# Weighted one-hot factors of the first prompt tile on GpSimd between its gathers, those of the second tile on VectorE

## The reference

```python
s1 = jnp.einsum('nhd,kd->nhk', q[..., :half], c1)
s2 = jnp.einsum('nhd,kd->nhk', q[..., half:], c2)
...
e = jnp.take_along_axis(cidx, si, axis=-1)
g = jax.nn.softmax(sv, axis=-1)
ue = u[e]
ve = v[e]
a = jax.nn.gelu(jnp.einsum('nhkd,nd->nhk', ue, hx), approximate=False)
return jnp.einsum('nhk,nhkd->nd', (g * a), ve)
```

## Time and the profile before

| | |
|---|---|
| median of 3 runs | 1579.57 us (1575.74 to 1583.34) |
| the profiled execution | 1577.69 us, its span 1575.9 us |
| PE busy | 1167.5 us (74%) |
| DVE busy | 1035.7 us (66%) |
| POOL busy | 646.8 us (41%) |
| ACT busy | 291.7 us (19%) |
| moved by DMA | 434.92 MB, mean 276 GB/s |

### The profile page before, as it was taken

One profiled execution on the slowest core, in us unless ns is written; L12 is line 12 of the kernel. 1 busy time (PEld: TensorE's weight loads), 2 busy tenths in 40 slices (PEclk: granted clock), 3 DMA queues, 4 the chain that ended last, 5 costly groups with the idle time before them and its releaser, 6 DMA issues.

```text
span 1575.9 us, 12501 instructions
## 1 busy us (share of the span) xinstructions
PE 1167.5 (74%) x4129; PEld 695.2 (44%) x4129; DVE 1035.7 (66%) x2220; ACT 291.7 (19%) x701; POOL 646.8 (41%) x565
## 2 busy tenths in 40 slices
PE   7999998975420683674586584027799999999998
PEld 3444444852110673673244374026544444444443
DVE  2436313579999878777447569999856566666664
ACT  2024501210000011111046441149600000000000
POOL 1110000333333757767324453445544454444451
PEclk9999999997755555555698777556799999999999
DMA  7654231684643988998987765656699999999996
GB/s 265 219 187 164 81 143 44 250 293 161 250 140 97 358 275 325 364 339 282 389 296 250 253 228 202 228 175 208 233 409 410 409 410 409 409 409 410 409 401 252
DMA packets 155361, 434.92 MB, mean 276 GB/s; under 512 B 14592, under 2 KB 36496, under 8 KB 155040
## 3 DMA queue, kind: packets, MB, share of 16 engines
q0 software_dynamic: 74688, 271.66, 46.8%
q1 hardware_dynamic: 80608, 162.45, 28.3%
HBM read 427.72 MB, written 6.34 MB: 275 GB/s over the span
## 4 chain that ended last, share of the span: by engine, by line
PE 56%; DVE 21%; DMA 9%; ACT 8%; issue 3%; POOL 3%; SPq 1%; DVEq 0%; ACTq 0%
PE wide L1189 28%; DVE rows_ring L1505 6%; PE accumB L873 5%; PE accumA L873 4%; DMA ring<-in_w_in 3%; DMA rows_ring<-in_peer_u,expert 3%; ACT hot L805 3%; POOL rows_ring L576 2%; PE wide L1079 2%; PE accumB L1101 2%; PE accumB L1135 2%; PE transB L849 2%; PE transB L1135 2%; PE wide L952 2%; PE wide L991 2%
## 5 line engine op out<-in xcount | busy, mean ns | idle before, releaser
L576 POOL DMA_INDIRECT rows_ring<-in_peer_u,expert x384 | 477.9, 1245 | 437.8 <-DVE dots L1505 351.0
L1505 DVE CUSTOM_DVE_ANT_0 rows_ring<-rows_ring,arena 128x1024 f32<-128x1024 f32 x384 | 458.6, 1223 | 125.4 <-DMA rows_ring<-in_peer_u,expert 123.0
L1189 PE MATMUL wide<-ring,arena 128*128 128x512 f32 x1024 | 439.7, 592 | 0.7 <-issue 0.7
L1189 PEld LDWEIGHTS wide<-ring,arena 128*128 128x128 f32 x1024 | 194.5, 190 | 245.3 <-issue 245.3
L1510 DVE SCALAR_TENSOR_TENSOR x<-rows_ring,dots,x 128x1024 f32<-128x1024 f32 x128 | 164.4, 1284 | 99.2 <-DMA rows_ring<-in_peer_v,expert 99.2
L576 POOL DMA_INDIRECT rows_ring<-in_peer_v,expert x128 | 127.1, 993 | 136.1 <-DVE x L1510 129.1
L849 PE MATMUL transB<-ident,arena 128*128 128x128 f32 x198 | 48.7, 389 | 126.8 <-DVE arena L1290 59.8
L873 PE MATMUL accumB<-ring,arena 128*128 128x512 f32 (+1 forms) x192 | 89.1, 622 | 56.9 <-ACT arena L651 50.0
L849 PEld LDWEIGHTS transB<-ident,arena 128*128 128x128 f32 x198 | 31.5, 195 | 141.3 <-DVE arena L1290 60.6
L873 PE MATMUL accumB<-arena 128*128 128x512 f32 x160 | 74.4, 620 | 23.9 <-ACT arena L651 12.3
L873 PEld LDWEIGHTS accumB<-ring,arena 128*128 128x128 f32 x192 | 40.0, 212 | 103.5 <-ACT arena L651 52.4
(11 more groups left out here) (218 smaller groups left out, 1418.0 us busy)
## 6 DMA issues: line engine op xcount, KB each, us to landing
ring<-in_peer_v SPq DMA_DIRECT2D x128, 512.0 KB, 6.8
ring<-in_w_in SPq DMA_DIRECT2D x10, 2048.0 KB, 10.2
arena<-in_w_in SPq DMA_DIRECT2D x10, 2048.0 KB, 8.8
ring<-in_w_pq SPq DMA_DIRECT2D x4, 2048.0 KB, 9.9
arena<-in_w_pq SPq DMA_DIRECT2D x4, 2048.0 KB, 8.9
arena<-in_w_out SPq DMA_DIRECT2D x3, 2048.0 KB, 10.3
rows_ring<-in_peer_u,expert POOLq DMA_INDIRECT x384, 6.8
arena<-in_w_br_a SPq DMA_DIRECT2D x2, 2048.0 KB, 7.6
```

What stands on the lines that cost most here:

```text
L576: pool.indirect_dma_start(rowbuf[:, n % ROWS, :], None, u_rows if n < U_ROWS else v_rows, index).then_inc(S(f"rows{n % ROWS}"), 16)
L1189: ins = pe.matmul(wide[:, 2 * t + half, :], dense[t][:, b, :], vblock[:, b % VBLOCKS, half * 512:half * 512 + 512], start=b == 0, stop=b = ...
L1505: v.tensor_tensor_reduce(row, row, h2[:, t, :], 1.0, 0.0, ALU.mult, ALU.add, dots[:, t, k:k + 1]).then_inc(S("row_used"), 1)
```

## The change

POOL makes the 32 groups of `hot1` of tile 0, at the same steps 47 to 57 and with the same two waits per group, after its gathers of the step. DVE makes those of tile 1 only. The waits differ in one place: POOL waits on `built` from its third group on as DVE did, and at its first group also for the rows of tile 0 having been read, since `hot1[0]` lies where their activations lay.

```diff
-            between = [laid(steps(G1))]
+            def dense_weights():
+
+                for g in range(TGROUPS):
+                    yield dense_at(0, g)
+                    if g == 0:
+                        pool.wait_ge(S("turned_copied"), 2)
+                        pool.wait_ge(S("row_used"), SLOTS)
+                    if g >= 2:
+                        pool.wait_ge(S("built"), g - 1)
+                    for j in range(TOKENS):
+                        tok = g * TOKENS + j
+                        ins = pool.tensor_scalar(hot1[0][:, g % 2, j * P:j * P + P], iota[:, :], turned[:, 0, tok:tok + 1],
+                                                 turned[:, 2, tok:tok + 1], ALU.is_equal, ALU.mult)
+                    ins.then_inc(S("hot1_ready"), 1)
+
+            between = [laid(steps(G1)), laid(dense_weights())]
...
             between = [laid(x) for x in (early(steps(G0)), route(0), route(1), steps(G1), route(SAMPLE), weights(0),
-                                         dense_weights(0), weights(1), dense_weights(1), weights(SAMPLE))]
+                                         weights(1), dense_weights(), weights(SAMPLE))]
```

More of the change, by code:

```diff
@@ L1479, in weights, with dense_weights @@
                     step(v.tensor_tensor(part, part, gate[:, t, q * w:q * w + w], ALU.mult), "weights_ready")
-            def dense_weights(t):
+            def dense_weights():
+                t = 1
                 for g in range(TGROUPS):
```

## The result

The changed kernel takes 1641.45 us (median of 4, 1636.13 to 1654.98), beside 1581.45 us for the kernel before in the same comparison. The ratio is 1.0395, with a 95% interval of 1.0364 to 1.0426. That is 60 us slower, where 24.4 were forecast, and outside the range of 1587 to 1626 us. The profiled execution is the slowest of the four, 1654.98 us with a span of 1653.2, 77.3 us above that of before. So the distance in the traces is some 17 us larger in all than that of the medians.

What follows compares the result with a forecast made beforehand. The prediction took a chain of waits, DVE's from the routing's start at 943.35 us, as the bound. Terms -3.7 + 3 x 7.7 + 5 = +24.4 us gave 1602.1 us, 1604.0 on the median, range 1587 to 1626.

Steps and rivals of the forecast that it cites:

- The sum of the order: Whole forecast: -3.7 + 3 x 7.7 + 5 = +24.4 us, from gathers standing behind POOL's waits on PE.
- the first loop: Step 53, the addition before PE's second output product: +7.7 us.
- the next two: Step 54, the addition before ACT's square, and step 55, `h2` before PE's turn: +7.7 us each.
- my 13.4: Loop from PE building a step's first group to DVE's last row of the next step: 13.4 us, before 5.7.
- the price of a group: POOL's four factors, 1.3 us, with 0.3 us for the wait in front: 1.6 us.
- the landing: Time from a gather's issue to its row landing, taken as 6.8 us, between 5.30 and 9.39.
- The gain of 4.5 us by an earlier load of the gate weights: Before 779 us: some 1.8 MB of rows less competing with weights PE waits for gives 4.5 us, 3.7 remaining after step 50.
- I take 0.32 us each: Cost of one of POOL's 128 factors, taken from the nearest passes over 128x128 at 284 and 344 ns.
- The factors on the path below run mostly when DVE has no row, so I stay near the passes.: POOL's factors on the path: claimed little stretched by DVE's rows, so kept near the 284 and 344 ns passes.
- The rival that came true: POOL itself becomes the bound: at 1.5 us per factor about +120 us, deciding from about 0.7 us; chance 0.08.
- Faster: Rival: next step's rows are in SBUF before POOL stalls, so -17 us, 1563 us; chance 0.08.
- no change: Rival: longer loops overlap uncounted work or weights' loads hide two, gain at step 47 whole: about +5 us, 1585 us; chance 0.12.

Runs made afterwards that it cites:

- one small operation per group: Changed kernel with one one-column factor per group on POOL instead of four of 128 columns, output wrong: 1600.55 us, ratio 1.0129, +21.5 us.
- The thin factors: Changed kernel with each of POOL's 128 factors made over 1 column instead of 128, order and waits kept, output wrong: 1614.53 us, ratio 1.0227.
- one small operation per group in the lagged order: Changed kernel with one one-column factor per group and POOL's groups one step later in its order, output wrong: 1566.44 us, ratio 0.9918.
- the third buffer: Kernel before, all factors on DVE, with a third factor buffer for the first tile in 512 free arena columns: 1558.32 us, ratio 0.9865.

## Why the prediction was wrong

**Right: the direction and the mechanism named.** The stall moved to POOL in front of the gathers, DVE waits 172.5 us for rows in the stretch to 1017 us (0.4 before, to 931), and the two waits for `x1` and `h2` grew by 7.1 and 7.7 us in the changed kernel and by 7.8 and 6.4 with one small operation per group. The sum of the order, +24.4 us, was measured as +21.5 by that run.

**Partly luck: how well the terms fit.** In that run the path reaches PE's turn of the merge 2.5 us earlier than before (3.7 predicted), the second output product 7.6 us later (4.0), `h2` 19.5 us later (19.4) and the routing 25.2 us later (24.4). So the first loop cost 10.1 us instead of 7.7 and the next two 11.9 instead of 15.4. A loop of 13.5 us (864.20 to 877.7) beside my 13.4 is made of other parts: from the build to the first gather it takes 0.6 us instead of 1.6, and the row lands 7.9 us after its issue instead of 6.8. In the changed kernel these are 3.4 and 5.6 us, and the loop is 14.0 us (916.3 to 930.3). Errors in the price of a group and in the landing cancelled. The gain of 4.5 us by an earlier load of the gate weights didn't come (0.05 and 0.7 us above).

**Wrong: "I take 0.32 us each".** The factor costs 0.80 us quiet and waiting for the one before, 0.78 in a run of them, and 1.05 on the mean of the changed kernel. I took the nearest passes by shape, 128x128, and none of them compares or reads per-partition scalars. That is two and a half times the price, before DVE. This is the term of the sum that failed.

**Wrong: "The factors on the path below run mostly when DVE has no row, so I stay near the passes."** True of the three groups that wait for PE at steps 53 to 55 (3.11 us for four factors), and beside the point: POOL's whole step counts once it is near PE's, and in each step DVE's four rows hold POOL up by 3.5 us. With 12 x 0.78 = 9.4, plus 3.5, plus 5.0 for the gathers it comes to 17.9 us; measured are 17.5 to 17.9.

**The rival that came true** had 0.08. Its threshold, 0.7 us per factor, was well placed in kind but too high. It left the 3.5 us out: with them a step reaches 13 us at (13 - 5 - 3.5) / 12 = 0.38 us per factor, and the measured 11.7 us at 0.27, by my estimate from these runs. That is below the 0.32 us that I had taken. The thin factors bear it out: 0.375 us each when quiet, near my price, and +35.3 us where one operation per group gave +21.5. So the forecast stood on the edge of a cliff, and the sum should have shown it: I compared POOL's step with PE's only at the rival's price.

**The sum isn't a sum.** Above one small operation per group in the lagged order, 1566.4, the order is worth 34 us and POOL's full length 69 us (1635.0), and the changed kernel has both at 75 us (1641.45). In most steps either the wait for PE or POOL's own work sets when the gathers go out, whichever is later. When factors are dear, the order still costs something only where POOL waits for PE, at steps 53 to 55, and that is the 6.4 us at most, if it is more than noise.

**Faster and no change** needed rows ahead of the stall. With one small operation and the groups a step later that is what happens, at -12.6 us beside the rival's -17.

Open: how much of the 77.3 us in the profiled execution, as against 60 in the medians, belongs to that execution alone. Its first factor starts at 789.79 us and DVE's first before the change at 790.24, so next to nothing of the gain at the load is seen in it. Also open is which of DVE's shorter waits make up the 20.7 us of the third buffer, as against 12.4 us of waits of PE for DVE. The other executions have no trace.

## What to carry to other kernels

Before work is moved to an engine that issues transfers, add up its whole step (transfers, work, and what another engine's operations take from it) and compare it with the step of the engine it must keep up with. A wait in front of transfers is paid with their whole latency, whereas in front of work on landed data it is paid with that work. Where one engine stalls on a double buffer with unrelated work queued behind, a third buffer can give more than another engine: here -20.7 us with 2 KB per partition, beside -12.6 us for taking the work off DVE at next to no cost elsewhere.

## What the runs showed of the hardware

- On GpSimd a tensor_scalar over some 125 columns of f32 takes 295 ns with add and multiply and immediates, and 651 ns with a compare in the add's place. Two per-partition scalars add some 150 ns to either. The same factor takes 352 ns on VectorE.
- A GpSimd factor that began beside VectorE's row operations (two inputs in SBUF, 1.22 us each) waited out two of them in a row: 2.48 us instead of 0.78.
- Gathers on GpSimd took 0.94 to 1.01 us in the changed kernel's steps, mostly ahead of VectorE's rows, and 1.68 to 1.99 us before beside its rows.
- The same 16 matmuls of 128x512 f32 of the gate projection took 9.75 us with a granted TensorE clock of 0.59 (779.4 to 786 us, before) and 7.10 us with 1.00 (one small operation per group).
